# Differential attention: one VectorE instruction for both score maxima of a unit instead of two

## The reference, cut to what matters

```python
def blocked_diff_attention(q, k, v, lam, scale):
    ...
    def one(qi):
        s = jnp.einsum('bqhnd,bkhnd->bhnqk', qi, k, ...) * scale   # n = 0, 1: two maps
        p = jax.nn.softmax(s, axis=-1)
        a = p[:, :, 0] - lam * p[:, :, 1]
        return jnp.einsum('bhqk,bkhe->bqhe', a.astype(v.dtype), v)
```

## Time and profile before

| what | value |
|---|---|
| median of three runs | 4802.51 us |
| the profiled execution | 4795.76 us |
| its span, first to last instruction | 4794.0 us |
| mean granted TensorE clock, share of full speed | 0.961 |
| PE busy | 4469.1 us (93%) |
| DVE busy | 2112.7 us (44%) |
| ACT busy | 1601.4 us (33%) |
| the chain that ended last | PE 85%, DVE 6%, ACT 3%, issue 3% |
| line 2024 (all maxima, of this stage and of the latent attention), x224 | 268.3 us busy |

### The profile page before, as it was taken

How to read it: one execution, slowest core, us unless ns; L and a number is a source line. 1 busy time by engine, 2 the same in 40 slices (tenths; PEclk the granted TensorE clock), 3 DMA queues, 4 the chain that set the end, 5 groups by cost and what they waited for, 6 DMA issues and landing times.

```text
span 4794.0 us, 53934 instructions
## 1 busy us (share of the span) xinstructions
PE 4469.1 (93%) x22204; PEld 3454.2 (72%) x22204; DVE 2112.7 (44%) x3237; ACT 1601.4 (33%) x2422; POOL 379.5 (8%) x397
## 2 busy tenths in 40 slices
PE   7999988999899898899899986999999999999999
PEld 7677655677777765667767345788888888888887
DVE  0334775543123576554333556433333453333344
ACT  0424654431132465443143642321122333112132
POOL 0101000000000100000000565100000220000010
PEclk9999999999599998999999997999999999999999
DMA  4011000011411100001111000111111111111112
GB/s 169 27 69 38 18 1 1 1 53 45 149 44 56 35 18 1 1 1 58 63 58 44 1 38 1 41 48 48 50 49 48 71 36 36 44 53 44 53 44 79
DMA packets 30092, 207.86 MB, mean 43 GB/s; under 512 B 4640, under 2 KB 4768, under 8 KB 9120
## 3 DMA queue, kind: packets, MB, share of 16 engines
q1 hardware_dynamic: 20880, 152.05, 8.9%
q10 hardware_dynamic: 8976, 52.47, 3.0%
HBM read 187.73 MB, written 12.58 MB: 42 GB/s over the span
## 4 chain that ended last, share of the span: by engine, by line
PE 85%; DVE 6%; ACT 3%; issue 3%; DMA 1%; DVEq 1%; POOL 0%; ACTq 0%; POOLq 0%; SPq 0%
PE ps L720 19%; PE ps L1198 11%; PE ps L1200 11%; PE ps L1199 11%; PE ps L692 4%; PE ps L1022 4%; PE ps L843 4%; PE ps L972 3%; PE ps L961 2%; PE ps L849 2%; PE ps L904 1%; PE ps L889 1%; PE ps L981 1%; PE ps L806 1%; PE ps L916 1%
## 5 line engine op out<-in xcount | busy, mean ns | idle before, releaser
L1198 PE MATMUL ps<-n_hi,w_hi 128*128 128x512 f32 x1280 | 500.1, 391 | 0.0
L1200 PE MATMUL ps<-n_hi,w_lo 128*128 128x512 f32 x1280 | 498.0, 389 | 0.0
L1199 PE MATMUL ps<-n_lo,w_hi 128*128 128x512 f32 x1280 | 497.9, 389 | 0.0
L1198 PE MATMUL ps<-m_hi,w_hi 128*128 128x512 f32 x1152 | 449.8, 390 | 0.0
L1200 PE MATMUL ps<-m_hi,w_lo 128*128 128x512 f32 x1152 | 448.2, 389 | 0.0
L1199 PE MATMUL ps<-m_lo,w_hi 128*128 128x512 f32 x1152 | 448.1, 389 | 0.0
L1344 ACT ACTIVATE w_hi<-w 128x2048 fp32r<-128x2048 f32 x92 | 176.0, 1913 | 476.1 <-DMA w<-in_wstream 475.9
L2024 DVE TENSOR_REDUCE small<-ps 128x1 f32<-128x1024 f32 x224 | 268.3, 1222 | 110.3 <-PE ps L1022 88.3
L2627 DVE TENSOR_TENSOR m<-ps,arena 128x512 f32<-128x512 f32 x128 | 88.5, 692 | 433.5 <-ACT arena L1861 433.5
L1199 PEld LDWEIGHTS ps<-n_lo,w_hi 128*128 128x128 f32 x1280 | 240.2, 188 | 50.9 <-issue 1.2
L1198 PEld LDWEIGHTS ps<-n_hi,w_hi 128*128 128x128 f32 x1280 | 240.3, 188 | 50.9 <-issue 1.2
(11 more groups left out here) (344 smaller groups left out, 8431.1 us busy)
## 6 DMA issues: line engine op xcount, KB each, us to landing
w<-in_wstream SPq DMA_DIRECT2D x145, 1024.0 KB, 4.8
h<-in_xT ACTq DMA_DIRECT2D x2, 4096.0 KB, 14.3
out<-h ACTq DMA_DIRECT2D x2, 4096.0 KB, 17.1
h<-out ACTq DMA_DIRECT2D x2, 4096.0 KB, 12.3
h<-in_na_bias ACTq DMA_DIRECT2D x6, 1152.0 KB, 7.0
out<-h ACTq DMA_DIRECT2D x16, 256.0 KB, 2.0
m<-arena ACTq DMA_DIRECT2D x8, 256.0 KB, 8.1
arena<-arena ACTq DMA_DIRECT2D x8, 256.0 KB, 4.0
```

The costliest lines, as they stand in the source:

```text
L1198: mm(dst, wb[0][:, k, wcols], hi[:, k, :], start=(g == 0), stop=False)
L1199: mm(dst, wb[0][:, k, wcols], lo[:, k, :], start=False, stop=False)
L1200: last = mm(dst, wb[1][:, k, wcols], hi[:, k, :], start=False, stop=(g == KT - 1))
```

## The change

In VectorE's loop the two calls of `maximum` are replaced by one wait and one instruction. The wait is for `s_full` of both maps of the unit. The instruction reads all four score banks, seen as 128 x 2 x 1024, reduces the last axis, and writes the two negated maxima side by side into `negm`, where the two calls wrote them. It raises `m_ready` by two when it is finished. `maximum` itself stays for the latent attention. TensorE's and ScalarE's code is the same, so the first exponential still waits for the first count of `m_ready` and the second for the second.

```diff
                     for c in range(U + 4):
                         if c < U:
-                            maximum(2 * c, psf[:, 0:2 * HALF])
-                            maximum(2 * c + 1, psf[:, 2 * HALF:4 * HALF])
+                            dve.wait_ge(sems["s_full"], T.since("s_full", 2 * c + 2))
+                            V.reduce_max(negm[:, 2 * c:2 * c + 2], psf[:, 0:4 * HALF].rearrange("p (i k) -> p i k", i=2),
+                                         AX.X, negate=True).then_inc(sems["m_ready"], 2)
                         if 1 <= c <= U:
```

## The result

The changed kernel took 4924.08 us in the median of four runs (4920.44 to 4930.23), against 4803.06 us (4797.46 to 4807.7, four runs): ratio 1.0254, 95% interval 1.0236 to 1.0272, or 121 us more. The forecast was 4900 with a range of 4880 to 4950. The profiled execution took 4923.52 us with a span of 4921.7, which is 127.7 us over the span of before; its mean granted clock is 0.946 instead of 0.961.

The account below looks back on a forecast made before the run. TensorE's 4.28 us and VectorE's 4.17 were taken to nearly fill each 4.34 us unit. Steady intervals 41.5 + 41.6, starts 8.7 + 5.1 and ends 2 x 1.07 add 99 us: 4902 from the median, stated as 4900, range 4880 to 4950.

Parts of the forecast that it names:

- The ring: Differential stage's steady state: maximum, both exponentials and scores of map 1 in series, 5.88 us a unit against 4.34.
- the clock: TensorE's clock in units 5 to 31 of each layer stays at its full level, adding nothing.
- rival B: TensorE's clock falls too, given its 0.77 us gap a unit: 8.05 us a unit there, 4940 or 5018; chance 0.12.
- third of the 54: Assumed share of the steady intervals at the lower clock: 18 x 2.17 = 39 us more, 4940.
- The reduction: On VectorE, one maximum of 2048 elements takes 2.29 us, where the two took 2.36 together.
- VectorE's saving: 0.07 us a unit, 4.5 us over 64, worth nothing if VectorE has time to spare afterwards.
- The stage's end: After each layer's last maximum the second exponential starts 1.07 us later, and what follows is the same.
- The fourth interval: At each layer's start, TensorE takes up the values as well at the low clock: 8.05 us.
- The first units: Units 0 to 4, at the lower clock, take 28.57 us: +8.7 in layer 1, +5.1 in layer 2.
- The slack of before: In the kernel before, one map's ring takes 3.68 us against 4.34 a unit, leaving 0.66 us.
- Rival A: VectorE holds the differential stage and its 0.07 us a unit saving counts: 4799 us; chance 0.05.
- Rival C: The second exponential's 1.13 us is hidden: +0.41 us a unit, about 4837 us; chance 0.03.

Follow-up runs that it names:

- The wait alone: Kernel before with the first maximum waiting for both maps' scores, the two maxima separate, each releasing its own exponential: 4842.86 us, ratio 1.0082.
- the release alone: Kernel before with each maximum keeping its own wait, but only the second releasing both exponentials at its end: 4851.68 us, ratio 1.0092.
- map 0 halved: Kernel before with the maximum of map 0 over its first 512 keys alone: 4785.25 us, ratio 0.9968.
- both halved: Kernel before with both maxima over the first 512 of the 1024 keys of their map: 4781.18 us, ratio 0.9954.
- map 1 halved: Kernel before with the maximum of map 1 over its first 512 keys alone: 4798.05 us, ratio 1.0.
- GpSimd's factors: Kernel before with reciprocals taken ahead of the next unit's maxima and GpSimd making the factor of the second map: 4808.57 us, ratio 1.0015.

## Why the prediction was right, and where it was short

The measured 4924 lies in the stated range but above the forecast's own, 4885 to 4915. The ring alone gives some 4900, as forecast. The rest is the clock, which the forecast put at nothing and for which the range had been widened by the near part of rival B. So the total is inside the range thanks to that allowance, and in part by luck: of rival B the price of a slow unit was twice too high, and its third of the 54 was an assumption, where 13 were hit. By the prediction's own sign, the clock leaving its full level between units 5 and 31, it was wrong on this term.

- *The ring.* Right in its mechanism and nearly in its size: 5.92 instead of 5.88. The wait alone and the release alone each give 4.8 to 4.9 us, and both together 5.92, with either form of the reduction. The terms: 2.33 as forecast, 1.10 for the first exponential (forecast 1.13), 1.25 as forecast, 1.24 from scores to reduction (forecast 1.17). I had the last one from a maximum over one map. It is not map 1 that makes it longer: two maxima that wait for map 1's scores start 1.18 after them, and the 1.24 comes with the instruction over both maps. TensorE's gap is 0.87 us and not 0.77, since the values start 0.18 before the reduction (609.93 and 610.11) and not with it.
- *The reduction.* 2.29 us, 64 times, from PSUM with two outputs as from SBUF with 32. VectorE's saving counts for nothing, as forecast.
- *The clock.* This is the term that was mis-sized. The forecast held it at nothing; rival B had 0.12 and a unit at the lower clock at 8.05 us. It happened, in 13 of 54 intervals, but each cost 1.1 us and not 2.2: the chain has slack on TensorE. In the unit of the reduction at 621.95 the scores come 1.35 instead of 1.25 us after the second exponential, behind transposes that take longer, and the next reduction 2.25 instead of 1.24 after the scores; the exponentials don't move. That makes 15 us. The stage's end took 8.6 over the forecast, 6.9 of it in layer 1, where it now runs at 0.50 as only layer 2's did. Forecast and rival B were not two cases; both came in part.
- *Why the clock was put at nothing.* The argument was that the new loop is denser than the end of layer 1's stage, which kept the full clock with PE busy for 3.42 of 5 us. That row is 5 us out of some 15 without scores, and layer 2's row, 3.89 of 5 us at 0.50, spoke against it. The changed loop, busy for 16.4 of 20 us, is denser than that row and lost the clock again and again over 160 us. So the busy share in that row was no guide.
- *The price of the lower clock in the units.* 8.05 was read off an interval in which TensorE was the limit. The changed kernel wasn't limited by TensorE, so that row didn't apply to it. The fourth interval, too, was 7.17 and 7.00 where I had put 8.05. The first units cost 12.0 us together instead of 13.8.
- *The slack of before.* I gave the rings 0.66 us of slack and took TensorE's chain, 4.28, as the limit. The runs with half the maxima disproved that: part of the 1.48 for scores in the earlier trace rows is a wait, and the earlier trace rows has one of two intervals that alternate (4.28 and 4.41). What sets 4.34 is a ring over two units: 3.64 from a first maximum to the scores of the next unit's map 1, then 3.87 on TensorE to the next scores of map 0, then 1.17: (3.64 + 3.87 + 1.17) / 2 = 4.34. It gives 4.08 for map 0 halved (measured 4.08), 4.08 for both halved (4.06), 4.34 for map 1 halved (4.33) and 4.34 for GpSimd's factors (4.34). For the sum of the forecast this made no difference, since 4.342 itself was measured.
- *Rival A* is out: the change made the kernel slower, and with 3.5 us in 40 less for VectorE nothing moved. *Rival C* is out: the interval is the full sum.
- *Open:* the 4.8 us outside the stage. The runs of one kernel spread by 10 us, so these can't be told from chance. What decides after how many units the clock falls wasn't tried either; it differs between the layers and between executions.

## What to carry to other kernels

One instruction for two saves some of its engine's time, here 0.07 us, and ties the waits and releases of the two together. Before joining, write down the ring of each part and then the ring of the joined one: here two rings of 3.68 became one of 5.92. And an engine that is 96% busy need not be the limit: move work off it, or change where its work stands, and look which of the two moves the time. Where a longer chain opens a gap on TensorE in each round, allow for its clock as well: here that was 15 us in the units on top of 85 for the chain.

## What the hardware showed that I had not expected

- TensorE's clock fell to 1.2 GHz in a loop whose longest gap at the full clock was about 0.9 us, with PE busy for 16.4 of 20 us, and stayed at 2.4 GHz when 0.88 us of repeated transposes filled that gap. The kernel with more work was 27 us faster (4897.69 against 4924.46).
- Two maxima of 1024 elements back to back, with no semaphore between, release what follows only 0.05 us later than one of 2048 (2.38 against 2.33 after the start). Counted from the scores that both wait for there is no difference (3.56 and 3.57), because the single one starts 0.06 later.
